# Memory's keys and values moved into the expert loop, interleaved entries, an early root on GpSimd

## What is computed

```
# first block, at the end of each layer: top 2 of 32 experts per token
x = x + hier_moe(rms_norm(x, ffn_norm[l]), ...)   # per expert: (silu(x@w1) * (x@w3)) @ w2, rows weighed
# at the start of each layer, and of the second block
h = rms_norm(x, gain);  proj = h @ w_in[l]
# second block, layer i: keys and values of the memory, which depend on no x at all
k, v = split(rms_norm(mem, mem_kv_g[i]) @ wkv[i], 2)      # wkv 1024 x 2048
```

## Time and profile before

| | |
|---|---|
| median of 3 runs | 3264.57 us (3264.05 to 3266.88) |
| the profiled execution: time, span | 3260.7 us, 3258.9 us |
| TensorE (PE) busy | 3016.8 us, 93% |
| VectorE, ScalarE, GpSimd busy | 744.8, 603.6, 336.2 us |
| expert loop, layer 0 and layer 1 | 375.9 to 628.6 us, 1031.3 to 1286.2 us |
| end of the loop to the next first product | 628.6 to 680.5 us, 1286.2 to 1338.7 us |

### The profile page before, as it was taken

How to read it: one execution, slowest core, us unless ns; L and a number is a source line. 1 busy time by engine, 2 the same in 40 slices (tenths; PEclk the granted TensorE clock), 3 DMA queues, 4 the chain that set the end, 5 groups by cost and what they waited for, 6 DMA issues and landing times.

```text
span 3258.9 us, 26999 instructions
## 1 busy us (share of the span) xinstructions
PE 3016.8 (93%) x10596; PEld 1536.1 (47%) x10596; DVE 744.8 (23%) x1730; ACT 603.6 (19%) x1288; POOL 336.2 (10%) x570
## 2 busy tenths in 40 slices
PE   7999877899998877999999999999998899999999
PEld 3465522344655323444664644444444564644444
DVE  3533311134333111213521100000116622100001
ACT  3332200123322000103512200000105422100000
POOL 2101111021011110001300000000003500000000
PEclk9999999899999999999999999999999999999999
DMA  3113599921135999421011222222220030222121
GB/s 139 46 46 149 217 420 414 366 102 46 46 145 197 420 418 362 157 78 52 16 63 52 75 73 73 75 78 77 78 78 27 1 103 27 77 78 77 65 103 52
DMA packets 111801, 421.02 MB, mean 129 GB/s; under 512 B 9008, under 2 KB 13104, under 8 KB 83888
## 3 DMA queue, kind: packets, MB, share of 16 engines
q1 hardware_dynamic: 98304, 381.94, 30.8%
q0 software_dynamic: 12784, 35.13, 2.8%
q10 hardware_dynamic: 576, 2.10, 0.2%
HBM read 408.64 MB, written 27.26 MB: 134 GB/s over the span
## 4 chain that ended last, share of the span: by engine, by line
PE 59%; issue 24%; DMA 10%; DVE 2%; POOL 2%; POOLq 1%; ACT 1%; SPq 0%; DVEq 0%; ACTq 0%
PE ps L402 15%; PE ps L2267 10%; PE ps L2538 9%; DMA ring_feat<-in_w 9%; PE ps L2606 5%; PE ps L1054 4%; PE ps L1563 3%; PE ps L2365 2%; PE ps L1603 2%; PE ps L2385 2%; PE ps L1810 1%; PE ps L1821 1%; PE ps L1833 1%; PE ps L691 1%; DMA tmp<-normed,route_i 1%
## 5 line engine op out<-in xcount | busy, mean ns | idle before, releaser
L2538 PE MATMUL ps<-ring_feat 128*128 128x512 f32 (+1 forms) x1536 | 605.2, 557 | 0.0
L2538 PEld LDWEIGHTS ps<-ring_feat 128*128 128x128 f32 x1536 | 291.5, 190 | 311.7 <-issue 305.2
L2267 PE MATMUL ps<-ring_feat 128*128 128x512 f32 x768 | 330.3, 592 | 0.0
L402 PE MATMUL ps<-ring_feat 128*96 128x512 f32 (+3 forms) x768 | 306.8, 556 | 4.4 <-DVE tmp L457 4.4
L2606 PE MATMUL ps<-ring_feat,tmp 128*128 128x512 f32 x704 | 302.8, 592 | 0.0
L2267 PEld LDWEIGHTS ps<-ring_feat 128*128 128x128 f32 x768 | 145.6, 190 | 181.8 <-issue 181.8
L402 PEld LDWEIGHTS ps<-ring_feat 128*128 128x128 f32 (+1 forms) x768 | 139.7, 184 | 156.6 <-issue 119.5
L2606 PEld LDWEIGHTS ps<-ring_feat,tmp 128*128 128x128 f32 x704 | 133.6, 190 | 167.4 <-issue 167.4
L2365 PE MATMUL ps<-ring_feat 128*128 128x512 f32 x448 | 194.6, 593 | 2.9 <-ACT ring_feat L2511 2.2
L1563 PE MATMUL ps<-ring_feat,tmp 128*64 128x512 f32 x512 | 129.0, 652 | 56.5 <-DMA ring_feat<-in_w 52.1
L1563 PE MATMUL ps<-big,tmp 128*64 128x512 f32 x512 | 122.7, 626 | 48.5 <-DMA big<-in_w 42.0
(11 more groups left out here) (369 smaller groups left out, 3212.2 us busy)
## 6 DMA issues: line engine op xcount, KB each, us to landing
big<-in_w SPq DMA_DIRECT2D x48, 2048.0 KB, 17.4
ring_feat<-in_w SPq DMA_DIRECT2D x48, 2048.0 KB, 18.6
ring_feat<-in_w_gate_up SPq DMA_DIRECT2D x22, 2048.0 KB, 8.1
ring_feat<-in_w_mix_in SPq DMA_DIRECT2D x12, 2048.0 KB, 8.1
ring_feat<-in_w_down SPq DMA_DIRECT2D x10, 2048.0 KB, 7.3
big<-in_w_mem_kv SPq DMA_DIRECT2D x6, 2048.0 KB, 20.6
ring_feat<-in_w_out SPq DMA_DIRECT2D x4, 2048.0 KB, 8.6
tmp<-expert_out SPq DMA_DIRECT2D x16, 512.0 KB, 4.5
```

The lines of the kernel that those rows point to most:

```text
L402: yield T.matmul(bank, lhs(k), rhs(k), start=k == 0, stop=k == n - 1)
L2267: yield T.matmul(bank, featv[:, k, t * P:(t + 1) * P], w[:, k, :], start=k == 0, stop=k == KC - 1)
L2538: m = T.matmul(bank[:, tokens], w[:, kk, o:o + P], featv[:, kk, tokens], start=kk == 0, stop=kk == KC - 1)
```

## The change

Chunk 1 of `w_mem_kv` is loaded right behind chunk 0, before the loop, into a place of its own (`kv_w`, 4096 columns of `tmp`, for which the routing's small tensors move elsewhere). Its four key jobs run one each at the start of pairs 2 to 5. Chunk 2 is loaded behind the loads of pair 7, and its two value jobs run in halves at the start of pairs 8 to 11. Chunk 3 is loaded behind those of pair 15, and its two jobs (`last_values`) stand on TensorE right behind the last down product, before the branch of `spilled`. The stores of chunks 1 and 2 are issued by GpSimd within the loop. GpSimd waits for the last scatters behind the branch instead of ahead of it, and takes one power of a constant after it has raised `rows_home`. At its very start it multiplies and takes a power of a constant. At the three entries only tile 0 is turned ahead of the first product; tiles 1 and 2 follow it, tile 3 follows the second one (at the second layer of the second block nothing is turned differently than before).

```diff
...
                     scale_x(eng, j + t, t, buf)
                 if name == "pool":
                     root_x(eng, j + t)
-            for t in range(TT - 1):
-                turn_x(name, eng, t)
+            turn_x(name, eng, 0)
         def rotate(dve, t1, t2, c, s, work, n):
...
-            for t in range(1, TT):
-                lat_tile(name, eng, l, t, w)
+            lat_product(name, eng, 0, w)
+            turn_x(name, eng, 1)
+            turn_x(name, eng, 2)
+            lat_read(name, eng, l, 0)
+            lat_product(name, eng, 1, w)
+            turn_x(name, eng, 3)
+            lat_read(name, eng, l, 1)
+            for t in range(2, TT):
+                lat_product(name, eng, t, w)
...
                 feat_free.append(count[("pe", "full")])
...
-        cand, e_left = view(tmp, R + 704, TT, N_EXP), view(tmp, R + 832, TT, N_EXP)
...
+        raw, biased = view(tmp, R_A, TT, LOGITS), view(tmp, R_A + 144, TT, LOGITS)
...
+        rev_of, blocks = view(tmp, R_C + 712, 2, TT), view(tmp, R_C + 720, N_EXP)
...
                 for t in range(MT):
-                    A.activation(view(tmp, (6 + t) * D, D), mem[:, t, :], ACT.Square, scale=float(D) ** -0.5,
+                    A.activation(view(wk, t * D, D), mem[:, t, :], ACT.Square, scale=float(D) ** -0.5,
                                  accum_out=mem_ss[:, t:t + 1]).then_inc(mem_squared, 1)
...
             o = PAR1["group_b"][0]
-            return rows[:, 0:KC * P] if c < 2 else par[l][:, o + (c - 2) * KC * P:o + (c - 1) * KC * P]
+            return rows[:, 0:KC * P] if c == 0 else par[l][:, o + c % 2 * KC * P:o + (c % 2 + 1) * KC * P]
...
                 eng.wait_ge(bank_full, f + 1)
-                if c == 1 and i == 0:
-                    eng.wait_ge(kv_stored, 16 * (4 * l + 1))
                 A.activation(kv_stage(l, c)[:, i * N_MEM:(i + 1) * N_MEM], bank, ACT.Copy).then_inc(bank_read_act, 1)
...
+            first, last = (0, KC) if part is None else (part * KC // 2, (part + 1) * KC // 2)
+            if first == 0:
+                at["value", name] = next_bank(name, "dve")
+            q, f = at["value", name]
             at["kv", c] = q
             bank = bank_of(q)
             if name == "pe":
-                pe_job(eng, q, product(bank, lambda k: memT[:, k, t * P:(t + 1) * P], lambda k: w[:, k, :], KC))
-            if name == "dve":
+                for k in range(first, last):
+                    m = T.matmul(bank, memT[:, k, t * P:(t + 1) * P], w[:, k, :], start=k == 0, stop=k == KC - 1)
+                if last == KC:
+                    m.then_inc(bank_full, 1)
+            if name == "dve" and last == KC:
+                if c == 3 and t == 0:
+                    eng.wait_ge(kv_stored, 16 * (4 * l + 3))
                 eng.wait_ge(bank_full, f + 1)
                 V.tensor_copy(kv_stage(l, c)[:, t * 512:(t + 1) * 512], bank).then_inc(bank_read_dve, 1)
...
-        def kv_chunk(name, eng, l, c):
-            w = view(big, (c - 1) * UP, KC, 512)
-            done_loads = 9 * (l + 1)
-            if name == "pe":
-                if c == 1:
-                    eng.wait_ge(hiddenT_ready, (l + 1) * PAIRS)
-                    set_ring(eng, 8)
-                if c == 3:
-                    eng.wait_ge(y_copied, (l + 1) * PAIRS)
-                eng.wait_ge((up_loaded[0] + down_loaded)[c - 1], 16 * done_loads)
-            if c == 1:
-                for i in range(4):
-                    key_job(name, eng, l, c, i, w)
-            else:
-                for t in range(MT):
-                    value_job(name, eng, l, c, t, w)
+        kv_w = view(tmp, 7 * D, KC, 512)
+        KEY_PAIRS, VALUE_PAIRS = range(2, 6), range(8, 12)
+        def load_kv(sp, l, c):
+            sp.dma_start(kv_w, a["w_mem_kv"][l][:, :, c * 512:(c + 1) * 512]).then_inc(kv_w_in, 16)
+        def pair_job(name, eng, l, p):
+            if p in KEY_PAIRS:
+                if name == "pe":
+                    eng.wait_ge(kv_w_in, 16 * (3 * l + 1))
+                key_job(name, eng, l, 1, p - KEY_PAIRS[0], kv_w)
+            if p in VALUE_PAIRS:
+                if name == "pe":
+                    eng.wait_ge(kv_w_in, 16 * (3 * l + 2))
+                t, part = divmod(p - VALUE_PAIRS[0], 2)
+                value_job(name, eng, l, 2, t, kv_w, part)
+        def last_values(name, eng, l, t):
+            if name == "pe" and t == 0:
+                set_ring(eng, (5, 3))
+                eng.wait_ge(kv_w_in, 16 * (3 * l + 3))
+            value_job(name, eng, l, 3, t, kv_w)
         def first_max(dve, src, n, hot, rev, work):
...
+            dve.wait_ge(bank_read_act, reads_of[at["memT"]]["act"])
             dve.drain()
...
+            dve.wait_ge(normed_out, 16 * (TT * l + TT - 1))
             rev = rev_of.rearrange("p i t -> p (i t)")
...
-            if p == PAIRS:
-                src = a["w_mem_kv"][l][:, :, (h + 1) * 512:(h + 2) * 512]
-                sp.dma_start(dst.rearrange("p (k n) -> p k n", k=KC), src).then_inc(up_loaded[0][h], 16)
-                return
             sp.dma_start(dst.rearrange("p (e n) -> p e n", e=2),
...
             dst = e_w[p % 2][:, 2 * UP:]
-            if p == PAIRS:
-                sp.dma_start(dst.rearrange("p (k n) -> p k n", k=KC), a["w_mem_kv"][l][:, :, 1536:2048]).then_inc(down_loaded[0], 16)
-                return
             sp.dma_start(dst.rearrange("p (e n) -> p e n", e=2),
...
                     sp.wait_ge(freed, l * PAIRS + p - 1)
                     load_up(sp, l, p, h)
                 sp.wait_ge(down_full, l * PAIRS + p - 1)
                 load_down(sp, l, p)
+                if p == KEY_PAIRS[-1] + 2:
+                    load_kv(sp, l, 2)
+            load_kv(sp, l, 3)
...
             g0 = l * PAIRS
-            turns, w_turns = PAIRS // 2 * l, ((PAIRS // 2 + 1) * l, PAIRS // 2 * l)
+            turns = PAIRS // 2 * l
...
                 for p in range(PAIRS):
+                    pair_job(name, eng, l, p)
                     if p + 2 < PAIRS:
                         gather_rows(p + 2)
                     store(p)
-                for s in range(2):
-                    eng.wait_ge(y_stored[s], 16 * (turns + PAIRS // 2))
-            if name == "pe":
-                reads_settled(name, eng)
+                    if p == KEY_PAIRS[-1] + 1:
+                        kv_store(eng, l, 1)
+                    if p == VALUE_PAIRS[-1] + 1:
+                        kv_store(eng, l, 2)
+            if name == "pe":
+                set_ring(eng, (5,))
                 turn_rows(0)
                 for p in range(PAIRS):
+                    pair_job(name, eng, l, p)
                     up(p)
                     if p:
...
+                for s in range(2):
+                    eng.wait_ge(y_stored[s], 16 * (PAIRS // 2) * (l + 1))
                 eng.nop().then_inc(rows_home, 1)
+                G.tensor_tensor(out=stat[:, 254:255], in0=c_("ones")[:, 0:1], in1=stat[:, 255:256], op=ALU.pow)
         combine_y = []
...
+                if name == "dve" and t == 1:
+                    last_values(name, eng, l, 1)
             return y0
...
+                    if c == 0 and t == 0 and l == 0:
+                        turn_x(name, eng, 1)
+                        turn_x(name, eng, 2)
+                    if c == 0 and t == (1 if l == 0 else 0):
                         turn_x(name, eng, TT - 1)
...
+                G.tensor_tensor(out=stat[:, 254:255], in0=stat[:, 255:256], in1=stat[:, 255:256], op=ALU.mult)
+                eng.drain()
+                G.tensor_tensor(out=stat[:, 254:255], in0=stat[:, 254:255], in1=stat[:, 255:256], op=ALU.pow)
...
-                    kv_store(eng, 0, 2)
...
                 experts(name, eng, l)
-                spilled(name, eng, l)
-                kv_chunk(name, eng, l, 1)
-                if name == "pool":
-                    kv_store(eng, l, 1)
+                if name != "pe":
+                    spilled(name, eng, l)
+                last_values(name, eng, l, 0)
+                if name != "dve":
+                    last_values(name, eng, l, 1)
+                if name == "pe":
+                    spilled(name, eng, l)
+                    eng.wait_ge(y_copied, (l + 1) * PAIRS)
+                    set_ring(eng, range(8))
                 arrived = combine(name, eng, l)
-                kv_chunk(name, eng, l, 2)
-                kv_chunk(name, eng, l, 3)
             if name == "dve":
                 eng.wait_ge(par2_loaded[0], 16)
...
                 load(a["w_mem_kv"][l][:, :, 0:512], KC, 512)
+                load_kv(sp, l, 1)
...
                 expert_loads(sp, l)
-                sp.wait_ge(down_full, (l + 1) * PAIRS)
                 spilled("sp", sp, l)
```

76 lines of the change are left out of this document (38 added, 38 removed).

## The result

The changed kernel takes 3236.63 us, median of 4 runs (3234.99 to 3239.07); the kernel before took 3264.31 us in 4 runs beside it (3260.77 to 3266.88). The ratio is 0.9917, with a 95% interval of 0.9899 to 0.9934: 27.7 us less, where the forecast had 24.2. The profiled execution took 3234.99 us against 3260.7.

A forecast was written before the change was run, and what follows sets the result against it. The expert loop was taken as bound by DMA bytes. Terms 13.1 + 11.3 - 0.2 gave 24.2 us less: 3236.5 for the profiled execution, 3240 us against the median, range 3226 to 3256.

The forecast's parts named there:

- Jobs in the loop: Expert loop: memory's key and value jobs fill TensorE's waits for weights, cost 0; upper bound 4 us a layer.
- Bytes in the loop: Expert loop: chunk 2's load adds 5.1 us and the stores of chunks 1 and 2 add 2.6, 7.7 a layer.
- Layer 0's boundary: From layer 0's loop to the next layer: lat products end at E+54.8 instead of E+75.6, 20.8 us less.
- E: The end of down(15), the expert loop's last product; E+25.9 means 25.9 us after it.
- Layer 1's boundary: From layer 1's loop to the second block: E+48.3 instead of E+67.3, 19.0 us less.
- The start: Program start: root 0 1.0 us later, the four lat products end 0.2 us later; bounds +1.5 and -3.3.
- The extra power behind `rows_home`: Behind layer 0's loop: it takes the 9.5 us stall between the first root's add and power, about E+7 to E+17.
- The early root: Rival, program start: the early pair ends GpSimd's hold sooner, first product 3.3 us earlier, 3237 us; chance 12%.
- The stall did not stay: Rival, layer boundaries: root stall remains, costing 2 to 3 us at layer 0, none to 1 at layer 1, 3243; 12%.
- The loop had no more room: Rival, expert loop: more room than thought, stores free and early DMA gaps used, 3235 us; chance 8%.
- TensorE did not become its bound: Rival, expert loop: TensorE becomes the bound, jobs add 27.5 us a layer, 31 us slower, 3295; chance 3%.
- Nothing ate the gain: Rival, whole kernel: a new wait eats the gain, time within 0.2% of before; chance 3%.

The follow-up runs named there:

- the cut products: Changed kernel with memory's in-loop products cut (key jobs 1 of 8, value parts 1 of 4), loads, copies and stores kept: 3235.92 us, ratio 0.9915.

## Why the prediction was right

The profiled executions differ by 25.7 us; the forecast's sum was 24.2. By its terms:

- **Jobs in the loop, cost 0: right,** and shown by the cut products (0.1 us).
- **Bytes in the loop, +7.7 a layer: right in sum** (+8.0 twice), in part by luck. The load costs 5.1 us for 1.84 MB, so 5.8 for its 2.1 MB, where 5.1 was taken (4.9 to 6.4 by the spread of the loops); the stores cost 0.9 to 1.6 where 2.6 was. That makes 6.7 to 7.4; some 0.6 to 1.3 us of the growth has no cause that a run shows, and it happens to fill the place of the stores' missing microsecond.
- **Layer 0's boundary, 20.8 less: 22.4.** First product E+25.1 (forecast 25.9), lat products' end E+53.2 (54.8). SyncE issued at E+5.0, not E+7.0, because the last store landed in 3.1 us, not the 4.3 taken from a gather. Tile 3's adds ended by E+22.0, not E+23.4. `w_lat` came last, as said.
- **Layer 1's boundary, 19.0 less: 20.0.** First product E+27.8 (28.5), third E+47.3 (48.3).
- **The start, +0.2: -0.3,** which single executions do not tell apart (they spread by 1.7 us there). Root 0 was 0.8 late (forecast 1.0), the first product at 21.57 (21.6).
- With the loops this gives 22.4 + 20.0 + 0.3 - 16.0 = 26.7 against the 25.7. The 1.0 us too much is placed by no row; TensorE's busy time is 2.1 us longer in the execution after, at a mean granted clock of 0.979 against 0.982.

**One step reached a right result by a wrong cause:** "The extra power behind `rows_home` takes that stall from about E+7 to E+17, so the roots are off the path." The roots were off the path, but the power ran at E+5.2 without a stall, and without it nothing changed. The stall had come with GpSimd's own store, and ended 1.6 us after that store's landing; moving the store into the loop is what shortened it. That the forecast of E+25.9 came out all the same is luck in this term: the move that did it was in the change for another reason. The row was in sight: GpSimd's timeline ahead of the earlier trace rows's root has the store of `mem_kv` right in front of it.

**The rivals.** The early root did not pay, and costs 0.8 us at the root. The stall did not stay. The loop had no more room than forecast. TensorE did not become its bound. Nothing ate the gain. The forecast also took the interleaved turns as a part of how the lat products came early; with the old order the time is the same, so this step too was not needed. And it read the hold at the start as bound to the instruction recorded at 14.8; the number was right, but the landing of GpSimd's own load fits the times of all 14 kernels.

## What to carry to other kernels

Where a loop is bound by bytes, look for products elsewhere that need nothing of its result, and put them into its waits: 26 to 30 us of TensorE's work in each loop cost nothing by itself; the loop grew by 8 us, most of it for the weights and stores that came along. Where several transfers and engines end almost together ahead of a product, read what comes second and third before moving the first; two earlier places for the weights' loads, and the turns moved behind the first product, gave nothing. And an idle time called "issue" on GpSimd is first to be looked for in its own queue: a small instruction behind a `drain` should not stand close behind a large load or store issued by GpSimd. At the start of this program GpSimd is held for some 12 us in this way; loading these parameters from another engine was not tried.
